# Splitting the per-head scaling of queries and keys between ScalarE and VectorE in a hybrid decoder layer

## The reference, cut to what matters

```python
h = rms_norm(x, norm1_g) * (1 + sc1) + sh1
z = h @ w_in
q, k, v, u = jnp.split(z, [ATTN_WIDTH, 2 * ATTN_WIDTH, 3 * ATTN_WIDTH], axis=-1)
q = rms_norm(q.reshape(B, T, N_ATTN_HEADS, HEAD_DIM), q_norm_g)
k = rms_norm(k.reshape(B, T, N_ATTN_HEADS, HEAD_DIM), k_norm_g)
```

## Time and profile before

| | us |
|---|---|
| median of 3 runs | 2871.91 (2870.61 to 2874.94) |
| the profiled execution, its own time | 2880.02 |
| its span in the trace | 2878.2 |
| stage of queries and keys, first matmul to first load of the next stage | 422.6 to 646.8 |

### The profile page before, as it was taken

The page is one execution under the profiler, slowest core; times in us unless marked ns, Lnnn a source line. Parts: engine busy times, 40 slices in busy tenths (PEclk is TensorE's granted clock), DMA queues, the critical chain, the costliest instruction groups (busy, mean ns, idle before and its releaser), DMA issues.

```text
span 2878.2 us, 46596 instructions
## 1 busy us (share of the span) xinstructions
PE 2703.0 (94%) x16354; PEld 2317.9 (81%) x16354; DVE 1578.9 (55%) x3774; ACT 1224.3 (43%) x3111; POOL 1315.5 (46%) x957
## 2 busy tenths in 40 slices
PE   6899989978999967999789999999999999999998
PEld 2688757865666643687589999999999999999998
DVE  3158889865666633787554444445444445444444
ACT  3334313445666632465444433444333344334432
POOL 0000000009999000566256655665656664557654
PEclk9999999988999988999899999999999999999999
DMA  7567535738545368457233324254222325413222
GB/s 260 194 216 244 200 109 199 242 118 242 175 155 177 118 229 324 140 189 245 89 122 130 93 84 138 74 172 165 77 86 94 122 84 183 151 59 110 82 74 78
DMA packets 322540, 434.71 MB, mean 151 GB/s; under 512 B 28202, under 2 KB 251802, under 8 KB 316158
## 3 DMA queue, kind: packets, MB, share of 16 engines
q1 hardware_dynamic: 299762, 341.21, 36.5%
q0 software_dynamic: 5072, 81.05, 7.9%
q10 hardware_dynamic: 17476, 9.47, 1.1%
HBM read 355.06 MB, written 148.74 MB: 175 GB/s over the span
## 4 chain that ended last, share of the span: by engine, by line
PE 40%; issue 2%; DVE 2%; DMA 2%; POOL 2%; ACT 1%; SPq 1%; DVEq 0%; POOLq 0%; ACTq 0%
PE ff_u_ps L2797 13%; PE ff_u_ps L2799 13%; PE ff_u_ps L2798 13%; POOL ff_w_lo L2444 1%; DMA gluT<-h_d 1%; DMA gluT<-in_w_ff_dram 1%; DMA out_y_prompt_dram<-ff_x_own 0%; POOL ff_a_lo L2459 0%; DVE ff_wT L2664 0%; ACT ff_w_hi L2502 0%; SPq L2367 0%; ACT ff_h_hi L2511 0%; POOL ff_h_lo L2453 0%; DMA ff_x_own<-x_d 0%; PE ff_out_ps L2792 0%
## 5 line engine op out<-in xcount | busy, mean ns | idle before, releaser
L2444 POOL TENSOR_TENSOR ff_w_lo<-gluT,ff_w_hi 128x512 fp32r<-128x512 f32 x342 | 464.2, 1366 | 299.0 <-ACT ff_w_hi L2502 298.6
L2797 PE MATMUL ff_u_ps<-ff_a_hi,ff_w_hi 128*128 128x352 f32 (+1 forms) x1536 | 495.8, 323 | 19.2 <-POOL ff_a_lo L2459 17.3
L2798 PE MATMUL ff_u_ps<-ff_a_lo,ff_w_hi 128*128 128x352 f32 (+1 forms) x1536 | 494.3, 322 | 0.0
L2799 PE MATMUL ff_u_ps<-ff_a_hi,ff_w_lo 128*128 128x352 f32 (+1 forms) x1536 | 494.3, 322 | 0.0
L2797 PE MATMUL ff_u_ps<-ff_h_hi,ff_w_hi 128*128 128x352 f32 (+1 forms) x1368 | 441.6, 323 | 18.0 <-DVE ff_h_lo L2612 9.6
L2799 PE MATMUL ff_u_ps<-ff_h_hi,ff_w_lo 128*128 128x352 f32 (+1 forms) x1368 | 438.6, 321 | 0.0
L2798 PE MATMUL ff_u_ps<-ff_h_lo,ff_w_hi 128*128 128x352 f32 (+1 forms) x1368 | 437.6, 320 | 0.0
L2701 DVE SCALAR_TENSOR_TENSOR ff_y<-ff_u_ps,modT,ff_y 128x352 f32<-128x352 f32 (+2 forms) x336 | 188.6, 571 | 375.9 <-PE ff_u_ps L2799 375.4
L2502 ACT ACTIVATE ff_w_hi<-gluT 128x512 fp32r<-128x512 f32 x342 | 210.2, 625 | 313.4 <-PE ff_u_ps L2799 274.9
L2444 POOL TENSOR_TENSOR ff_w_lo<-ff_wT,ff_w_hi 128x512 fp32r<-128x512 f32 x168 | 228.0, 1358 | 241.6 <-ACT ff_w_hi L2502 145.1
L2797 PEld LDWEIGHTS ff_u_ps<-ff_a_hi,ff_w_hi 128*128 128x128 f32 x1536 | 291.2, 190 | 24.0 <-POOL ff_a_lo L2459 21.3
(11 more groups left out here) (315 smaller groups left out, 5212.6 us busy)
## 6 DMA issues: line engine op xcount, KB each, us to landing
gluT<-in_w_ff_dram SPq DMA_DIRECT2D x192, 512.0 KB, 5.0
out_new_k_sample_dram<-in_cache_k_dram POOLq DMA_DIRECT2D x8, 4088.0 KB, 15.5
out_new_v_sample_dram<-in_cache_v_dram POOLq DMA_DIRECT2D x8, 4088.0 KB, 16.8
dwq<-in_w_ada_dram SPq DMA_DIRECT2D x32, 512.0 KB, 6.8
gluT<-in_cache_k_dram SPq DMA_DIRECT2D x16, 1024.0 KB, 11.6
sa_vn<-in_cache_v_dram SPq DMA_DIRECT2D x16, 1024.0 KB, 14.2
gluT<-h_d SPq DMA_DIRECT2D x80, 176.0 KB, 3.9
mx_acc<-acc_d SPq DMA_DIRECT2D x16, 768.0 KB, 8.0
```

The source lines that it names most:

```text
L2444: pool.tensor_tensor(slot_view(w_lo, s), src, slot_view(w_hi, s).bitcast(F32), ALU.subtract).then_inc(w_lod, 1)
L2797: pe.matmul(out, w_hi[:, s % WR, w], hi, start=first, stop=False, skip_group_check=more)
L2798: pe.matmul(out, w_hi[:, s % WR, w], lo, start=False, stop=False, skip_group_check=more)
L2799: return pe.matmul(out, w_lo[:, s % WR, w], hi, start=False, stop=last, skip_group_check=more)
```

## The change

ScalarE scales the eight query heads alone. VectorE takes the eight key heads from PSUM with one operation per head that multiplies by `rsq` and by the gain, in place of its one multiplication in `nrm`. `key_gain` therefore takes over the two waits on the free half of `nrm` and a wait for `rs_done`; `nrm_done` no longer implies that the queries are scaled, so TensorE waits for both counters. The last hunk of VectorE's loop moves `key_gain` of the last tile ahead of convolution operations of which that tile has none.

```diff
@@ scaled(u), ScalarE
-                            for h in range(2 * H):
-                                z = z_ps[(2 * u + h // H) % 6][0:n, h % H * DH:(h % H + 1) * DH]
+                            for h in range(H):
+                                z = z_ps[(2 * u) % 6][0:n, h * DH:(h + 1) * DH]
                                 ins = act.activation(nrm[0:n, u % 2, h * DH:(h + 1) * DH], z, ACT.Copy, scale=rsq[0:n, u % 2, h:h + 1])
                             ins.then_inc(z_free, 1)
@@ VectorE
                         def key_gain(u):
                             n = rows_of(tile_at[u])
-                            v.wait_ge(z_free, u + 1)
-                            k_rows = nrm[0:n, u % 2, AW:].rearrange("p (h d) -> p h d", d=DH)
-                            v.tensor_tensor(k_rows, k_rows, kgain[0:n].unsqueeze(1).to_broadcast([n, H, DH]), ALU.mult).then_inc(nrm_done, 1)
+                            if u >= 2:
+                                v.wait_ge(t_pe, 2 * (u - 1))
+                                v.wait_ge(k_out[u % 2], k_stored(u - 2))
+                            v.wait_ge(rs_done, u + 1)
+                            for h in range(H):
+                                z = z_ps[(2 * u + 1) % 6][0:n, h * DH:(h + 1) * DH]
+                                ins = v.scalar_tensor_tensor(out=nrm[0:n, u % 2, AW + h * DH:AW + (h + 1) * DH], in0=z, scalar=rsq[0:n, u % 2, H + h:H + h + 1],
+                                                             in1=kgain[0:n], op0=ALU.mult, op1=ALU.mult)
+                            ins.then_inc(nrm_done, 1)
@@ VectorE's loop over u
                             head_norms(u)
+                            if u == NT:
+                                key_gain(u)
                             for o in range(QK_OPS * u // (NT - 1), QK_OPS * min(u + 1, NT - 1) // (NT - 1)):
                                 late_op(v, cstep, o)
-                            key_gain(u)
+                            if u < NT:
+                                key_gain(u)
@@ products(u), TensorE
                                 if u >= 3 and c == 0:
                                     pe.wait_ge(z_free, u - 2)
+                                    pe.wait_ge(nrm_done, u - 2)
@@ turn_qk(u), TensorE
                             n = rows_of(tile_at[u])
+                            pe.wait_ge(z_free, u + 1)
                             pe.wait_ge(nrm_done, u + 1)
```

## The result

The changed kernel is slower by 0.18%: the ratio to the kernel before is 1.0018, with a 95% interval of 1.0011 to 1.0025. The medians are 2876.94 us (20 runs, 2872.76 to 2884.98) and, run beside them, 2873.11 us for the kernel before (20 runs, 2868.16 to 2877.57). The forecast was 2869.5 us, 0.08% faster.

The account below looks back on a forecast made before the run. TensorE was taken as the bound, at 11.77 us a tile. Steady tiles 0 and tail -2.4 us take the profiled 2880.0 to 2877.6, or the median 2871.9 to 2869.5 us; range 2865.5 to 2877.

Parts of the forecast that it names:

- The price of the operation: VectorE's new 64-column key operation: 281 ns each, 0.20 us from start to start, 1.7 us for eight.
- The pessimistic rule of the Trainium skill: VectorE's pipe must empty between operations; taken strictly, no overlap at 0.28 us each and 2872 us in all.
- VectorE fits under TensorE: Steady tiles: VectorE's period becomes 11.47 us against TensorE's 11.77, so TensorE is not held up, at a price of nothing.
- Covered by 1.6 us at its thinnest: Tile 1: its keys come at 474.0 us, before turn 1 at 475.59, the smallest margin of the steady tiles.
- The tail: Last tile: `nrm_done` and `store_k(16)` come earlier, so the chain to the next stage's loads moves by 2.4 us.
- I cost this move at nothing: Sync queue in steady tiles: stores issued later because VectorE is late were claimed to cost 0 us.
- one queue served in order: Sync queue: tile 1's store could not land before the load issued ahead of it, so issuing it later costs nothing.
- late stores: Rival, chance 0.10: landings move with issue, delaying turns 4 and 7 by 1.6 and 2.3 us; net +1.5, 2873.4 us.

Follow-up runs that it names:

- e2: Changed kernel, with GpSimd's second cache copy also waiting until tile 0's two stores have landed; ratio 1.0002 to the kernel before.
- e11: Kernel before, with only tile 14's stores issued ahead of tile 16's key store in the sync queue; ratio 0.9986 to the kernel before.
- e5: Kernel before, with only the second cache copy starting half a tile sooner, ahead of tile 0's key store; ratio 0.9995 to the kernel before.
- e3: Kernel before, with the change made in the last tile alone; ratio 0.9996 to the kernel before.
- e10: Kernel before, with the change in the last tile alone and tile 14's stores issued ahead of tile 16's key store; ratio 0.9988 to the kernel before.
- e1: Changed kernel run again without any edit; ratio 1.0014 to the kernel before.
- e7: Changed kernel, with the last tile as in the kernel before; ratio 1.0024 to the kernel before.
- e6: Kernel before, with one useless VectorE addition of 896 columns a tile in front of the key multiplication; ratio 1.0017 to the kernel before.
- e9: Kernel before, with tile 0's two small stores held for the count of products that releases the second cache copy; ratio 1.0019 to the kernel before.

## Why the prediction went wrong, point by point

**The price of the operation: right.** 0.20 us from start to start and 281 ns each were forecast; 0.19 and 275 ns came. The fixed costs read off rows of 352 and 1024 columns carried over to 64. The pessimistic rule of the Trainium skill (VectorE: DVE Perf Modes, the section on the DRAIN you can't avoid), that the next operation starts only when the pipe is empty, does not hold here as strictly as I took it, with durations that add up: eight operations of 275 ns took 1.62 us. The same section limits its rule itself: a next operation that is not held starts earlier.

**VectorE fits under TensorE: right for the period, wrong for the start.** The period was 11.39 us a tile against 11.77, forecast 11.47. "Covered by 1.6 us at its thinnest" was not so: tile 1's keys were ready at 471.09, 0.34 us ahead of turn 1, and turn 0, which I did not look at, waited 0.45 us for VectorE. The loss from turn 1 on does not come from this: e2 has the same wait and no loss there.

**The tail: right.** -2.32 forecast as -2.4, with the chain as described: `store_k(16)` behind eight operations, and the landing of tile 14's store releasing `turned(16)` at 642.99, 10.24 behind turn 14 instead of 12.56. The sync queue's own part in it (e11) I had named but not priced.

**The step that failed: "I cost this move at nothing".** I saw that VectorE's lateness moves every store of the sync queue, and then looked at the two stores for which ScalarE had waited before (`turned(3)` and `turned(6)`, tiles 1 and 4). The store that mattered had not been waited for in the profile before, because it had just got ahead of the copy: tile 0's, issued 3.8 us before it and landing in 2.2 us. By my own numbers the third `nrm_done` would come 2.4 us later, which leaves 1.4. The rows to see this stood in the timeline of the two queues; I did not compare a moved transfer with the transfers that it might fall behind. My reason for the zero, one queue served in order, looks at the sync queue's own transfers alone; what decided was a copy of GpSimd's queue. The move cost 8.27 us between turns 1 and 14.

That margin was also read from a lenient execution. From the reduction of tile 1 to turn 1 the kernel before has 13.59 us in its first profile; e5, e11 and e3, whose tiles are the old ones there, have 12.26, 11.57 and 12.20, and the store is 1.78 to 2.40 ahead in e3, e10 and e11. From 420 to 440 us TensorE's granted clock was 0.63 in that first profile and 0.81 to 0.89 in e3, e5, e10 and e11, so in that first profile TensorE arrived later against VectorE's fixed chain. With a margin of about 2.2 us and a shift of 2.4, the store lands on the edge, and did so in each of the three executions of the changed steady part with the copy and the order of `key_gain` untouched (0.16 to 0.19 us ahead at issue). In all three, turn 0 had waited for VectorE (0.45, 0.35 and 0.28 us in the changed kernel, e1 and e7). That ties TensorE, whose products release the copy, to VectorE, whose counter releases the store, and can explain why the distance is so nearly the same each time.

**The rival "late stores"** had the right mechanism at the wrong place, with its price too small. Turns 4 and 7, where it was priced, were never held up. It priced idle time only; here 6.41 us of idleness cost 8.27, since TensorE then ran at the lower clock. Its chance of 0.10 was far too low: a store's landing was taken to move with the issue by a few us, where next to a 4 MB copy it jumps by 14.6.

**Left open.** How often an execution of the changed kernel stops is not shown: all profiled ones did, and the times of its 20 runs spread over 12.2 us, those of the kernel before over 9.4. Why the loads of some stages later take some us more or less was not looked into.

## What to carry to other kernels

When an edit makes an engine later without making it the bound, list every transfer queued behind it and ask of each which big transfer it now comes before or behind, and not only how much later it goes; the waits that the old profile does not show, because they were won by 2 us, are the ones to look for. Compare the margin in more than one execution if the start of the stage is ragged. Look at the packets as well as at the bytes: a small store of many small packets has most to lose beside a copy of large ones. And put a result that a queue waits for ahead of the filler work on its engine: that alone turned the change from 1.0018 to 0.9987.

## What the runs showed of the hardware that I had not expected

A small store and a large copy from two queues did not share the DMA engines evenly. Tile 0's key store of 64 KB, issued from 0.2 us before to 0.4 us after a copy of 4 MB, landed 15.1 to 16.6 us after the copy was issued (after, e1, e6, e7, e9), which is when the copy itself landed (16.2 us in the changed kernel). The query store, issued 0.6 us sooner each time, took 2.1 us where that put it 0.60 to 0.80 us ahead of the copy, and 14.9 us in e9, where it was 0.22 us ahead.

The Trainium skill (DMA: Bandwidth & Descriptors, on queues, rings and completion order) says that each DMA engine takes turns between its queues, a packet at a time. The traces agree. These lines are from the view of DMAs of e1 (per queue: packets, MB, share of the 16 DMA engines), from 485 to 494 us, while the copy runs, and then the sync queue's line from 494 to 496 us:

```profile
q0 software_dynamic: 48, 3.14, 101.5%
q1 hardware_dynamic: 48, 0.01, 0.4%
```

```profile
q1 hardware_dynamic: 563, 0.40, 73.6%
```

By their bytes, q0 carries the copy, in packets of 65 KB, and q1 is the sync queue, whose 48 packets here are all under 512 B. They go one for one, in three bursts of 16 and 16 some 3 us apart. The key store alone has about 500 such packets: in the kernel before, the two stores make 1072 packets under 512 B between 483.4 and 486.5 us. So in turns with packets of 65 KB it gets only 48 packets through in 9 us; of the 563 from 494 to 496 us, when the copy's large packets are done, some 480 are small. The changed kernel shows the same from 488 to 496 us: 47 packets of the copy and 47 small ones.
